# Expert weights on other load semaphores, five norms summed on GpSimd, and another order at the kernel's end

## The reference

```python
h = h + spatial_gating(u, vv, c_w_s[j], c_b_s[j]) @ c_w_out[j]
h = h + moe_swiglu(rms_norm_2(h, ln_ffn[i]), router_w[j], moe_w1[j], moe_w3[j], moe_w2[j])
gate = jax.nn.sigmoid(rms_norm_2(h, ln_ple[i]) @ ple_gate[i])
h = h + gate * (p[i] @ ple_proj[i])
...
return rms_norm_2(h, final_norm)
```

## Time and profile before

| what | value |
|---|---|
| median of 3 runs | 2185.34 us |
| the profiled execution: time, span | 2185.26 us, 2183.3 us |
| PE busy | 2047.2 us, 94% |
| DVE, ACT, POOL busy | 1359.1, 917.0, 32.9 us |
| chain that ended last, on PE | 91% |
| mean granted TensorE clock | 0.966 |
| HBM read | 448.21 MB |

### The profile page before, as it was taken

One profiled execution on the slowest core, in us unless ns is written; L12 is line 12 of the kernel. 1 busy time (PEld: TensorE's weight loads), 2 busy tenths in 40 slices (PEclk: granted clock), 3 DMA queues, 4 the chain that ended last, 5 costly groups with the idle time before them and its releaser, 6 DMA issues.

```text
span 2183.3 us, 28927 instructions
## 1 busy us (share of the span) xinstructions
PE 2047.2 (94%) x12175; PEld 1832.8 (84%) x12175; DVE 1359.1 (62%) x1676; ACT 917.0 (42%) x1052; POOL 32.9 (2%) x74
## 2 busy tenths in 40 slices
PE   4988999879999999999999969999999999999987
PEld 3876888667778887899998859899999999898966
DVE  6779768541374134566532248787878787888852
ACT  1511111112125112343422247666767666666652
POOL 2000000000000000000000000000000000000000
PEclk8989899989999999999999969999999999999998
DMA  9835421323333243165763049898989999999960
GB/s 311 272 116 163 127 78 59 116 78 116 116 116 102 92 149 104 59 193 177 195 217 126 4 180 365 317 362 315 359 319 348 332 331 349 332 352 332 344 242 20
DMA packets 225579, 452.22 MB, mean 207 GB/s; under 512 B 6928, under 2 KB 91160, under 8 KB 225448
## 3 DMA queue, kind: packets, MB, share of 16 engines
q1 hardware_dynamic: 222128, 445.44, 58.0%
q0 software_dynamic: 1632, 4.75, 0.8%
q10 hardware_dynamic: 1688, 0.15, 0.1%
HBM read 448.21 MB, written 2.10 MB: 206 GB/s over the span
## 4 chain that ended last, share of the span: by engine, by line
PE 91%; DVE 5%; ACT 2%; DMA 1%; issue 1%; ACTq 0%; DVEq 0%; SPq 0%
PE bank L990 23%; PE bank L1929 15%; PE bank L1016 11%; PE bank L2139 10%; PE bank L833 5%; PE bank L868 3%; PE bank L647 3%; PE bank L1898 2%; PE bank L757 2%; PE bank L961 1%; PE bank L1967 1%; PE bank L968 1%; DVE arena L2836 1%; PE bank L1001 1%; DVE arena L2837 1%
## 5 line engine op out<-in xcount | busy, mean ns | idle before, releaser
L1684 DVE TENSOR_TENSOR ring_r<-ring,his_r 128x2816 fp32r<-128x2816 f32 (+1 forms) x192 | 587.3, 3086 | 57.3 <-ACT his_r L1296 57.2
L1296 ACT ACTIVATE his_r<-ring 128x2816 fp32r<-128x2816 f32 (+1 forms) x192 | 491.0, 2560 | 209.5 <-DMA ring<-in_moe_w_dram 200.2
L990 PE MATMUL bank<-his_r,hg_r 128*128 128x352 f32 x2048 | 355.5, 326 | 0.8 <-ACT hg_r L1317 0.8
L990 PEld LDWEIGHTS bank<-his_r,hg_r 128*128 128x128 f32 x2048 | 332.9, 188 | 1.9 <-issue 0.9
L2139 PE MATMUL bank<-hT,ring 128*128 128x256 f32 x912 | 217.1, 395 | 14.4 <-DVE arena L2682 10.8
L2139 PEld LDWEIGHTS bank<-hT,ring 128*128 128x128 f32 x912 | 176.6, 198 | 43.1 <-issue 18.3
L990 PE MATMUL bank<-ring_r,hg_r 128*128 128x352 f32 x1024 | 186.1, 324 | 0.0
L1929 PE MATMUL bank<-arena,ring 128*128 128x256 f32 x800 | 178.4, 380 | 1.8 <-ACT cw L1238 0.7
L1929 PEld LDWEIGHTS bank<-arena,ring 128*128 128x128 f32 x800 | 151.6, 190 | 22.9 <-ACT cw L1238 1.0
L990 PEld LDWEIGHTS bank<-ring_r,hg_r 128*128 128x128 f32 x1024 | 169.2, 188 | 0.0
L1929 PE MATMUL bank<-hT,ring 128*128 128x256 f32 x624 | 143.3, 386 | 4.8 <-ACT hT L2447 4.0
(11 more groups left out here) (482 smaller groups left out, 2518.1 us busy)
## 6 DMA issues: line engine op xcount, KB each, us to landing
ring<-in_moe_w_dram SPq DMA_DIRECT2D x128, 1408.0 KB, 8.1
ring<-in_moe_w_dram SPq DMA_DIRECT2D x48, 1536.0 KB, 9.2
ring<-in_even_w_in_dram SPq DMA_DIRECT2D x28, 1024.0 KB, 6.4
ring<-in_ada_w_dram SPq DMA_DIRECT2D x24, 1024.0 KB, 9.1
ring<-in_ffn_w_dram SPq DMA_DIRECT2D x22, 1024.0 KB, 5.4
ring<-in_odd_w_in_dram SPq DMA_DIRECT2D x9, 2048.0 KB, 7.7
ring<-in_moe_w_dram SPq DMA_DIRECT2D x16, 1024.0 KB, 7.3
ring<-in_a_w_in_dram SPq DMA_DIRECT2D x6, 2048.0 KB, 8.0
```

Of the source, the lines that this page charges most:

```text
L990: ins = mm(bank[first + m][:, 0:WC], x[:, KT // 2 * late + k, :], w[:, k, WC * m:WC * m + WC], start=(not late and k == 0 and s == "hg_hi" ...
L1296: A(moe_hi(n), moe_w(n), ACT.Copy).then_inc(sem("moe_hi"), 1)
L1684: V.tensor_tensor(moe_lo(n), moe_w(n), moe_hi(n).bitcast(F32), ALU.subtract).then_inc(sem("moe_lo"), 1)
```

## The change

1. The experts' chunks use load semaphores 4, 5, 1, 2, 3 in place of 0 to 4, at the same addresses.
2. For norms 2, 3, 4, 5 and 7 (`ADDED`) POOL adds the 8 squared tiles up with 7 in-place adds of 128x256, each behind its square and each waiting for the one before; PE runs one ones-matmul for the norm, where `norm_rest` stood.
3. The number of rounds is loaded once on each engine, and the loop becomes three `If`s, each with its own copy of the body.
4. At the end: `pg1` uses two banks; ACT writes `H2 = xT * gain` for each tile; PE turns it to token-major unscaled, behind the tiles of `pg1`; the reciprocal of norm 8 is turned into columns and applied by ACT in the evictions; each of four evictions has its own store of 256 KB. The reciprocal of norms 4 and 7 goes to a place of its own (`RPG`).

```diff
         for n in range(NE * PER):
-            place("moe", n, moe_at(n), n % MRING)
+            place("moe", n, moe_at(n), (4, 5, 1, 2, 3)[n % MRING])
...
+        ADDED = {2: 1, 3: 2, 4: 3, 5: 4, 7: 5}
...
-        def over_round(eng, r, body):
-
-            n = eng.value_load(OVERI[0:1, 0:1], min_val=0, max_val=ROUNDS)
-            with eng.If(n > r):
-                body()
+        def over_count(eng):
+
+            eng.wait_ge(sem("over_ready"), 1)
+            return eng.value_load(OVERI[0:1, 0:1], min_val=0, max_val=ROUNDS)
+
+        def over_rounds(eng, n, body):
+
+            for r in range(ROUNDS):
+                with eng.If(n > r):
+                    body(r)
...
-            sp.wait_ge(sem("toks_taken"), TK_OUT + 4)
-            sp.dma_start(out[0].rearrange("(u p) n -> p u n", p=P), OT[:, :, :]).then_inc(sem("stored"), 16)
-            sp.wait_ge(sem("stored"), 16)
+            for b in range(4):
+                sp.wait_ge(sem("toks_taken"), TK_OUT + b + 1)
+                half = slice(512 * (b % 2), 512 * (b % 2) + 512)
+                sp.dma_start(out[0, P * (b // 2):P * (b // 2) + P, half], OT[:, b // 2, half]).then_inc(sem("stored"), 16)
+            sp.wait_ge(sem("stored"), 64)
...
+            def add_up(i):
+                for q in range(1, KT):
+                    pool.wait_ge(sem("norm_squares"), KT * i + q + 1)
+                    ins = pool.tensor_tensor(NSQ[i][:, 0, :], NSQ[i][:, 0, :], NSQ[i][:, q, :], ALU.add)
+                    if q < KT - 1:
+                        step(ins)
+                ins.then_inc(sem("norm_added"), 1)
+
...
+            over = over_count(pe)
             scatter_main(NE - 1)
             pe_gemm("pp1", lambda k: PPT[2 + k], [(sem("ys_taken"), 2 * NE)])
             pe.wait_ge(*took("pp1", 8))
...
-            pe.wait_ge(sem("over_ready"), 1)
-            with pe.Fori(0, ROUNDS) as r:
-                over_round(pe, r, lambda: over_expert(r))
-            pe_gemm("pg1", h, [], ready=xg_waits(7), lead=2, mid=lambda: norm_rest(7, KT), between=norm_behind(8, all_of=True))
-            tokens(TK_OUT, [(sem("h_ready"), KT * 4)], lambda b, j: hT[:, 4 * (b % 2) + j, (b // 2) * P:(b // 2 + 1) * P], 4)
+            over_rounds(pe, over, over_expert)
+            def beside_pg1(q):
+                norm_behind(8, 3)(q)
+                if q >= 3:
+                    token_turn(q - 3, 8, H2)
+
+            pe_gemm("pg1", h, [], ready=xg_waits(7), lead=2, banks=2, mid=lambda: norm_rest(7, KT), between=beside_pg1)
+            norm_rest(8, 3)
+            for ct in range(KT - 3, KT):
+                token_turn(ct, 8, H2)
+            pe.wait_ge(sem("norm_scaled"), 2 * KT + 5)
+            for tt in range(TT):
+                ins = mm(bank[5][:, tt:tt + 1], nr[:, tt * P:(tt + 1) * P], ident[:, 0:1], start=True, stop=True)
+            ins.then_inc(sem("router_ready"), 1)
...
+            act.wait_ge(sem("router_ready"), 3)
+            A(RSC, bank[5][:, 0:TT], ACT.Copy).then_inc(sem("pair_rooted"), 1)
+            act.wait_ge(sem("pair_rooted"), 3)
+            act.wait_ge(sem("toks_ready"), TK_OUT + 4)
+            for b in range(4):
+                A(OT[:, b // 2, 512 * (b % 2):512 * (b % 2) + 512], bank[(2, 3, 6, 7)[b]][:, :], ACT.Identity, scale=RSC[:, b // 2:b // 2 + 1])\
+                    .then_inc(sem("toks_taken"), 1)
...
+            if i in ADDED:
+                if q == KT - 1:
+                    nc.tensor.wait_ge(sem("norm_rooted"), i)
+                    nc.tensor.wait_ge(sem("norm_added"), ADDED[i])
+                    nc.tensor.matmul(bank[4][:, 0:T], ones[:, :], NSQ[i][:, 0, :], start=True, stop=True).then_inc(sem("norm_summed"), 1)
+                return
```

More of the change, by code:

```diff
@@ L495, in finish_sync @@
         def finish_sync(sp):
-            sp.wait_ge(sem("over_ready"), 1)
+            n = over_count(sp)
             sp.wait_ge(*took("pp1", 8))
[L498 to L508, removed]
@@ L509, in finish_sync, with over @@
-            sp.wait_ge(sem("toks_taken"), TK_OUT + 4)
-            sp.dma_start(out[0].rearrange("(u p) n -> p u n", p=P), OT[:, :, :]).then_inc(sem("stored"), 16)
-            sp.wait_ge(sem("stored"), 16)
+            def over(r):
+                e = sp.value_load(OVERI[0:1, r + 1:r + 2], min_val=0, max_val=NE - 1)
+                sp.wait_ge(sem("psel_ready"), 4 * (r + NE) + 2)
+                for j in range(UPS + DOWNS):
+                    if j >= RING:
+                        sp.wait_ge(sem("moe_acc"), PER * (r + NE) + j - RING + 1)
+                    k, n_ = moe_shape(j)
+                    sp.dma_start(OSLOT[j % RING][:, 0:k * n_].rearrange("p (k n) -> p k n", k=k), moe_src(j, e))\
+                        .then_inc(sem(f"loaded_{j % RING}"), 16)
@@ L514, in build @@
+            over_rounds(sp, n, over)
+            for b in range(4):
[3 more added lines that the diff above has]
+            sp.wait_ge(sem("stored"), 64)
         TK_P, TK_W, TK_V, TK_H, TK_OUT = 16, 18, 20, 24, 28
@@ L1236, in act_rest @@
                 act.wait_ge(sem("toks_ready"), TK_P + 1 + i)
-                A(PPT[2 * i], bank[7][:, 0:T], ACT.Copy).then_inc(sem("ppt_half"), 1)
+                A(PPT[2 * i], bank[7][:, 0:T], ACT.Copy)
                 A(PPT[2 * i + 1], bank[7][:, T:2 * T], ACT.Copy).then_inc(sem("toks_taken"), 1)
@@ L1291, in hi @@
             def hi(n):
-                act.wait_ge(sem(f"loaded_{n % MRING}"), phases["moe"]["place"][n]["value"])
+                act.wait_ge(sem(f"loaded_{phases['moe']['place'][n]['sem']}"), phases["moe"]["place"][n]["value"])
                 if n >= HSLOTS:
@@ L1362, in act_rest @@
             take_gemm(act, "pp1", lambda q, lin, b: A(PP1[:, q, :], b, ACT.Copy))
-            act.wait_ge(sem("over_ready"), 1)
-            with act.Fori(0, ROUNDS) as r:
-                over_round(act, r, lambda: over(r))
+            over_rounds(act, over_n, over)
             act.wait_ge(sem("moe_done"), 1)
@@ L1376, in act_rest @@
                     act.wait_ge(sem("embedded"), KT + q)
+                    A(H2[:, q - 1, :], xT[:, q - 1, :], ACT.Identity, scale=col("fnorm", q - 1)).then_inc(sem("xg_ready"), 1)
                     square(8, q - 1)
             root(8)
-            def tokens(n0, dst):
-                for b in range(4):
-                    act.wait_ge(sem("toks_ready"), n0 + b + 1)
-                    A(dst[:, b // 2, 512 * (b % 2):512 * (b % 2) + 512], bank[b][:, :], ACT.Copy).then_inc(sem("toks_taken"), 1)
-            tokens(TK_OUT, OT)
+            act.wait_ge(sem("router_ready"), 3)
[5 more added lines that the diff above has]
+                    .then_inc(sem("toks_taken"), 1)
         def dve_rest(dve, V, ch, step, norm):
@@ L1636, in ple @@
                 dve.wait_ge(sem("norm_rooted"), nrm + 1)
-                step(V.reciprocal(nr[:, :], nr[:, :]))
+                step(V.reciprocal(RPG, nr[:, :]))
                 if i:
@@ L1644, in add @@
                     V.tensor_tensor(xT[:, q, :], xT[:, q, :], PG[:, q, :], ALU.add).then_inc(sem("embedded"), 1)
[L1646 removed]
+                take_gemm(dve, f"pg{i}", lambda q, lin, b: V.tensor_tensor(PG[:, q, :], b, RPG, ALU.mult), banks=(4, 2)[i],
                           between=lambda q: add(q - 1) if q else None)
@@ L1804, in over @@
                 V.memset(NEG[:, 0:1], 0.0)
-            dve.wait_ge(sem("over_ready"), 1)
-            with dve.Fori(0, ROUNDS) as r:
-                over_round(dve, r, lambda: over(r))
+            over_rounds(dve, over_n, over)
             V.memset(NEG[:, 1:2], 0.0).then_inc(sem("moe_done"), 1)
@@ L1811, in dve_rest @@
             ple(1, 7)
-            dve.wait_ge(sem("embedded"), 2 * KT)
-            norm(8, lambda ct: col("fnorm", ct), dst=hT)
+            dve.wait_ge(sem("norm_rooted"), 9)
+            V.reciprocal(nr[:, :], nr[:, :]).then_inc(sem("norm_scaled"), 1)
         def dve_angles(dve, V, ch, step):
```

26 lines of the change are left out of this document (17 added, 9 removed).

## The result

The changed kernel takes **2166.56 us** (median of 4 runs, 2166.48 to 2168.52), beside 2185.11 us (4 runs, 2183.87 to 2186.28) of the kernel before in the same measurement: ratio 0.9919, 95% interval 0.9907 to 0.9931. That is 18.6 us less. The prediction said 2152 us with a range of 2144 to 2158. The sign was right; the gain is little more than half of the 33.4 us forecast, and the time lies outside the range.

A forecast was written before the change was run, and what follows sets the result against it. PE was busy 94% of the span, so removed matmuls or PE waits were counted as gains. 18.4 + 11.4 - 3.7 + 1.5 + 5.8 = 33.4 us off 2185.3 gave 2152 us, range 2144 to 2158.

The forecast's parts named there:

- Load semaphores: End of cout and router stage: 13.3 us from ACT's wait plus 5.1 at full clock, 18.4 us gained.
- Rival (c): Router stage: the clock falls all the same, or the DVE part grows; 5 us less gain, 2157 us; chance 0.05.
- rival (d): End of cout: something else holds ACT's casts, so the 18.4 us stay; 2170 us; chance 0.03.
- Branches: Between pp1 and pg1: PE's three branches all stall at 3.86 us each, so pg1 starts 3.7 us later.
- rival (a): Between pp1 and pg1: only the first of PE's branches stalls, 7.4 us earlier; 2144.5 us; chance 0.15.
- Norms 2 to 5: Seven ones-matmuls fewer each, 12.0 us, less 0.6 waiting for POOL at norm 2: 11.4 us gained.
- `pg1`: Matmul stage pg1: norm's ones-matmuls saved, partly lost to a two-bank wait ahead of tile 2; 1.5 us gained.
- The end: From pg1's last tile to the end of the span: 12.3 us instead of 18.2, 5.8 us gained.
- The experts' stage: Experts' stage, over 800 us: taken to keep its length; a change would show the prediction wrong.

The follow-up runs named there:

- the run with the early load: Changed kernel with POOL's load of the router's weights waiting for cin's last read, not cout's 8 tiles; 2158.73 us, ratio 0.9887.
- the order of the turns: Changed kernel with early load of the router's weights and PE's turn of the reciprocal moved ahead of the last token turns; 2158.42 us, ratio 0.9882.
- the best kernel: Changed kernel plus early router-weights load, nested branches, reciprocal's turn moved ahead, POOL adding six squares with a second ones-matmul; 2148.70 us, ratio 0.9836.
- a fourth kernel: Changed kernel plus early router-weights load, nested branches, earlier reciprocal turn, six POOL squares with a second ones-matmul; 2148.70 us, again 2149.86 us.

## Why the prediction was wrong, and where it was right

**Load semaphores: the step that failed.** The first half was exact: 13.3 us for ACT's wait, whose square now ends 0.85 us after the last addition. The second half rested on "Without that wait PE comes from `cout` without a pause, so I take the stage at the full clock". This is wrong twice. First, a transfer issued by POOL at `cout`'s end had been hidden behind ACT's square, which came 13.3 us late: issued at 1254.07 and 6.9 us on its way, it was there before PE asked at 1268.83. Once ACT was on time, this load ended last, and PE waited 5.31 us. The prediction held ACT's root and DVE's reciprocal against the time at which PE wants them, but not the other semaphore that PE passes ahead of the router, `rw_loaded`. Second, even without a gap the clock fell 4.2 us after `cout`'s last addition, in the run with the early load. Of the 18.4 us, 7.9 were there; the early load brought the stretch down by another 7.9 (16.7 to 8.8), and the order of the turns together with a later fall of the clock by 3.0 more (to 5.9). Of the 10.5 us that are missing in this stage, 5.3 are PE's wait for the load, 2.5 more came back with it, since PE then began the router at the full clock, and 2.7 are left by the fall of the clock under work (8.8 us where 6.1 were forecast). Rival (c) had the fall of the clock, at 5 in 100; rival (d) had "something else holds", but put it on the casts, at 3 in 100. No rival had a load for which PE itself waits.

**Branches: right mechanism, size off.** The choice between one stall and three came out as argued, and rival (a) is dead: 3.57, 4.74 and 5.01 us. The size taken, 3.86 for each, was the one row at hand; in five executions of kernels with written-out bodies the first took 3.4 to 3.7 and the two that follow 4.7 to 5.2 each. `pg1` starts 5.4 us later, not 3.7. Why the later ones cost more was not tried. The choice of three was argued from one row that could not decide it, as the prediction says itself. The Trainium skill (Runtime: NRT & Kernel Launch, "Instruction fetch mechanics") says that a taken branch out of the held pages stalls for one fetch. The single branch over three bodies (3.83 us) against three branches (13.3 us) agrees with it, and so do the two loop branches of 0.23 us between places already visited.

**Norms 2 to 5: right, 1.3 us too much.** A step was 0.79 us against the 0.75 chosen; norm 2's wait was 1.04, predicted 0.6, and norms 3 to 5 had none. Nearly all of the 1.3 us that is missing went elsewhere: 2.4 us had been won at the start of attention 2 (813.36 to 810.91) and 1.0 was left 28 us later (841.29 to 840.30), because the clock stood at 0.63 there in place of 0.79 (before, then with the change):

```profile
830.00:838.00 8.00, 6.04 (x21) 4.79 (x22) 4.08 (x11) 2.98 (x10) 0.00 (x0) 0.79 0.70 258
...
830.00:838.00 8.00, 8.00 (x26) 6.04 (x25) 3.03 (x9) 2.18 (x8) 0.00 (x0) 0.63 0.42 158
```

Whether that is the additions' doing stays open: the same 32 matmuls took 8.86 us in the kernel before, 9.79 in the change and 7.17 without the additions, but 8.36 in the run with the early load, which has them too.

**`pg1`: 1.5 predicted, 0.4 measured.** Its 24 matmuls of the head took 8.27 us in place of 7.49, since more of them ran at 1.2 GHz. That isn't tied to the change either: the same 24 took 6.80 in one execution of the best kernel and 8.39 in another.

**The end: right.** 12.3 predicted, 12.5 measured. The experts' stage kept its length to 0.1 us.

Put together, 33.4 - 18.6 = 14.8 us are missing: 10.5 in the router stage, 1.7 in the branches, 1.3 in the norms, 1.1 in `pg1` and 0.2 at the end. One step makes seven tenths of the error, and the range was too narrow because that step had been given a width of 5 us at a chance of 0.05.

## What to carry to other kernels

When a long wait is taken away, list every semaphore that the waiting engine passes in the next stage, and look up when each would have been signalled had it not been for the wait: the next late thing is hidden in the old trace, and its row (a small load, issued at the stage's end) shows no wait at all. Load small tables when their address is free, not when the stage begins. Where a rarely taken path is written out several times, nest the tests so that the usual case takes one branch: three in a row cost PE 13.3 us, one over all of them 3.8.

## What the runs showed of the hardware

- The granted clock fell to 1.2 GHz while PE was busy without one gap: in four executions of three kernels during the router's matmuls, whose results have eight columns, 4.2 to 5.1 us after `cout`'s last addition; in two of a fourth kernel 6.6 us after it, in the transposes behind them. In both kernels looked at twice it did so at the same distance from `cout`'s end to 0.05 us, though the end itself moved by 3 to 4 us. Not explained.
- An addition on POOL takes 0.72 us alone. In norm 4, four that met VectorE's 3.09 us subtraction took 2.88 to 2.94 us: the one shown began 0.75 us behind it and ended 0.60 us after it. One in norm 3 that met a subtraction of 2.28 us took 1.79 and ended 0.58 us after it. The Trainium skill (SBUF — State Buffer, "SBUF: two separate sides") describes this as an exclusive lock of a shared pair of ports: a VectorE operation with two SBUF inputs that starts first holds it for its whole length against a GpSimd operation that reads SBUF. The rows agree; no run here took the meeting away. It cost nothing, since norm 4's sum wasn't due.
- The load of the router's 32 KB from POOL's queue took 6.5 to 6.9 us from issue to landing in all eleven kernels, at `cout`'s end as well as 35 us ahead of it. The DMA engines were nearly full with expert weights at the time (share 0.97 in the kernel before and in the run with the early load). The Trainium skill (DMA: Bandwidth & Descriptors, "Anatomy of one DMA — SWDGE (gpsimd) path") fits loads from this queue as about 2.0 us and the bytes over 436,000 per us, an estimate of 2.1 us for this one. The measurement decides: 6.6. In the changed kernel four loads of 128 and 256 KB from the same queue, issued at 445.6 to 447.5 when the DMA engines had been nearly idle (share 0.04), took 3.1 to 4.2 us. So size does not explain the 6.6; the busy engines may, which no run tried.
- The distance of a jump made no difference: PE's branch took 3.4 to 3.8 us over three bodies and 3.4 to 3.9 over one. A second and a third, taken right behind it to new places, took 4.7 to 5.2 each.
